# The first feed-forward layer of a two-block model as seven quarter products per weight panel

## What is computed

```python
x = x + jnp.concatenate([mix, mem_out], axis=-1) @ w_out[layer]
u = rms_norm(x, norm_ffn_g[layer]) @ w_ff1[layer]          # 1024 -> 4096
x = x + jnp.square(jax.nn.relu(u)) @ w_ff2[layer]          # 4096 -> 1024
```

## Time and profile before

| what | value |
|---|---|
| median of three runs | 1949.53 us |
| lowest and highest run | 1947.63 and 1950.62 us |
| span of the profiled execution | 1949.5 us |
| PE busy | 1872.8 us (96%) |
| DVE busy | 923.3 us (47%) |
| ACT busy | 741.2 us (38%) |
| POOL busy | 235.6 us (12%) |
| first product of the feed-forward layer | 457.4 us |
| last product of the feed-forward layer | 817.9 us |

### The profile page before, as it was taken

One profiled execution on the slowest core, in us unless ns is written; L12 is line 12 of the kernel. 1 busy time (PEld: TensorE's weight loads), 2 busy tenths in 40 slices (PEclk: granted clock), 3 DMA queues, 4 the chain that ended last, 5 costly groups with the idle time before them and its releaser, 6 DMA issues. The chain is left out here.

```text
span 1949.5 us, 32648 instructions
## 1 busy us (share of the span) xinstructions
PE 1872.8 (96%) x13677; PEld 1529.4 (78%) x13677; DVE 923.3 (47%) x1380; ACT 741.2 (38%) x1208; POOL 235.6 (12%) x295
## 2 busy tenths in 40 slices
PE   7999989889999999999999899999999999999998
PEld 6777877757888888778866688888888888888888
DVE  4446766555433444466368564343322763433223
ACT  6633444343321232245358453322222552222222
POOL 4012656410000000000124100000130000000000
PEclk9999999999999999999989999999999999999999
DMA  5222000012322322362100213223233113232222
GB/s 183 87 80 72 4 3 3 12 44 89 106 87 90 105 87 87 99 125 87 44 1 2 66 66 108 87 91 104 75 112 95 52 63 102 87 107 77 87 92 71
DMA packets 152069, 147.97 MB, mean 76 GB/s; under 512 B 13533, under 2 KB 149883, under 8 KB 151931
## 3 DMA queue, kind: packets, MB, share of 16 engines
q1 hardware_dynamic: 151804, 145.91, 23.8%
q10 hardware_dynamic: 126, 0.04, 0.0%
HBM read 143.84 MB, written 2.10 MB: 75 GB/s over the span
## 5 line engine op out<-in xcount | busy, mean ns | idle before, releaser
L243 DVE TENSOR_TENSOR weight_low<-weight_ring,weight_high 128x2048 fp32r<-128x2048 f32 (+2 forms) x141 | 301.1, 2135 | 482.6 <-ACT weight_high L234 482.5
L234 ACT CAST weight_high<-weight_ring 128x2048 fp32r<-128x2048 f32 (+2 forms) x141 | 249.9, 1773 | 320.6 <-PE psum L263 320.0
L261 PE MATMUL psum<-tail_operand_high,weight_high 128*128 128x512 f32 (+1 forms) x768 | 292.9, 381 | 8.6 <-DVE tail_operand_low L2815 7.9
L263 PE MATMUL psum<-tail_operand_high,weight_low 128*128 128x512 f32 (+1 forms) x768 | 290.7, 378 | 0.0
L262 PE MATMUL psum<-tail_operand_low,weight_high 128*128 128x512 f32 (+1 forms) x768 | 290.7, 378 | 0.0
L261 PE MATMUL psum<-tail_hidden_high,weight_high 128*128 128x512 f32 (+1 forms) x520 | 183.2, 352 | 2.5 <-DVE tail_hidden_low L3290 2.5
L263 PE MATMUL psum<-tail_hidden_high,weight_low 128*128 128x512 f32 (+1 forms) x520 | 182.7, 351 | 0.0
L262 PE MATMUL psum<-tail_hidden_low,weight_high 128*128 128x512 f32 (+1 forms) x520 | 182.6, 351 | 0.0
L261 PEld LDWEIGHTS psum<-tail_operand_high,weight_high 128*128 128x128 f32 x768 | 145.7, 190 | 39.9 <-issue 5.9
L262 PEld LDWEIGHTS psum<-tail_operand_low,weight_high 128*128 128x128 f32 x768 | 145.8, 190 | 29.8 <-issue 0.5
L263 PEld LDWEIGHTS psum<-tail_operand_high,weight_low 128*128 128x128 f32 x768 | 145.8, 190 | 29.4
(11 more groups left out here) (441 smaller groups left out, 3140.0 us busy)
## 6 DMA issues: line engine op xcount, KB each, us to landing
weight_ring<-in_w_ff SPq DMA_DIRECT2D x32, 1024.0 KB, 5.2
weight_ring<-in_ffn_w_gate SPq DMA_DIRECT2D x22, 1024.0 KB, 5.1
weight_ring<-in_ffn_w_up SPq DMA_DIRECT2D x22, 1024.0 KB, 5.1
weight_ring<-in_ffn_w_down SPq DMA_DIRECT2D x16, 768.0 KB, 4.4
weight_ring<-in_rw_in SPq DMA_DIRECT2D x11, 1024.0 KB, 5.1
weight_ring<-in_ffn_w_down SPq DMA_DIRECT2D x16, 640.0 KB, 3.9
weight_ring<-in_attn_w_in SPq DMA_DIRECT2D x9, 1024.0 KB, 5.4
weight_ring<-in_w_out SPq DMA_DIRECT2D x4, 1024.0 KB, 5.0
```

The source lines that it names most:

```text
L234: act.copy(self.w_hi[:, slot, 0:n], self.ring[:, slot, 0:n]).then_inc(self.panel_high, 1)
L243: dve.tensor_tensor(self.w_lo[:, slot, 0:n], self.ring[:, slot, 0:n], self.w_hi[:, slot, 0:n], ALU.subtract).then_inc(self.panel_low, 1)
L261: pe.matmul(out, w_hi, x_hi, start=start, stop=False)
L263: return pe.matmul(out, w_lo, x_hi, start=False, stop=stop)
```

## The change

The two multiplications of the feed-forward layer are done by a scheme of Strassen's kind (the form with seven products and fifteen sums). A panel of weights is seen as a 2x2 matrix of quarters (two blocks of input channels by two blocks of 128 output columns), the operand likewise (two blocks of channels by two halves of 256 tokens). Seven products of quarters take the place of eight.

- `Sevens` handles one panel. POOL forms four sums of quarters of the raw weights, each 128x512 (`sum_first`, `sum_second`). ACT and DVE split seven quarters and sums instead of four quarters, in four groups: 512, 1024, 1024 and 1024 columns. PE makes 7 x 4 x 3 = 84 matrix multiplications of 256 columns, in the order c = 0 to 6. ACT copies three partial results out of PSUM (`keep_first`, `keep_second`, `keep_third`), DVE adds the rest to them (`add_12`, `add_22`, `add_11`, `finish_21`). Products 2, 3 and 4 wait for the copies (`kept`), product 6 for `add_22` (`read`).
- `Turner` does the same for an operand: POOL forms four sums of quarters (128x256 each) in `turn`, ACT and DVE split seven quarters in groups of 3 and 4.
- `FirstOutput` takes the place of `project_add` for `w_out`, and makes the operand of the layer in turned form.
- `FeedForward` runs 32 panels in the order of `ffn_order`: four chunks, each of four input panels (each makes 256 hidden channels) and four output panels. For an output panel DVE scales the result (`finish_21`, `finish_22`, `finish_first`) and POOL adds it to the residual (`add_out`, two instructions of 128x512).
- The panels of `w_ff2` are now 8 blocks of rows by 256 columns per chunk. The number of weight bytes is the same.

The core of the diff (constructors, memory placement, the removed bodies of `project_add` and `squared_relu_in` and the unchanged `NormOperand` left out):

```diff
+PRODUCT_SLOT = (0, 2, 3, 5, 4, 6, 7)
+PRODUCT_GROUP = (0, 1, 1, 2, 2, 3, 3)
+PRODUCT_OPERAND = (0, 3, 4, 2, 5, 1, 6)
+PRODUCT_BANK = (0, 2, 0, 2, 0, 1, 0)
...
+    def sum_first(self, pool, pos):
...
+        self.landed(pool, pos)
+        if pos:
+            pool.wait_ge(self.low, 3 * (pos - 1) + 2)
+        pool.tensor_tensor(s1, raw[:, 0, 1], raw[:, 1, 1], ALU.add).then_inc(self.summed, 1)
+        pool.wait_ge(self.summed, 4 * pos + 1)
+        pool.tensor_tensor(s2, s1, raw[:, 0, 0], ALU.subtract).then_inc(self.summed, 1)
+
+    def sum_second(self, pool, pos):
...
+            pool.wait_ge(self.low, 3 * (pos - 1) + 3)
+        pool.tensor_tensor(s3, raw[:, 0, 0], raw[:, 0, 1], ALU.subtract).then_inc(self.summed, 1)
+        pool.wait_ge(self.summed, 4 * pos + 2)
+        pool.tensor_tensor(s4, raw[:, 1, 0], s2, ALU.subtract).then_inc(self.summed, 1)
...
+    def products(self, pe, pos, operand, claim):
...
+        for c in range(7):
+            claim(pe, c)
+            if c in (0, 1, 3):
+                pe.wait_ge(self.low, 3 * pos + PRODUCT_GROUP[c] + 1)
+            if c == 5:
+                pe.wait_ge(self.k.panel_low, self.g0 + pos + 1)
+            if c in (2, 3, 4):
+                pe.wait_ge(self.kept, 3 * pos + c - 1)
+            if c == 6:
+                pe.wait_ge(self.read, 4 * pos + 2)
+            slot = (self.base + PRODUCT_SLOT[c]) % 8
+            for kk in range(kp):
...
+                pe.matmul(out, w, x_hi, start=kk == 0 and not opened, stop=False, skip_group_check=opened)
+                pe.matmul(out, w, x_lo, start=False, stop=False, skip_group_check=opened)
+                last = pe.matmul(out, self.w_lo[:, slot, kk, :], x_hi, start=False, stop=kk == kp - 1, skip_group_check=opened)
+            last.then_inc(self.k.panel_used if c == 6 else self.done, 1)
...
+    def turn(self, pool, q, first_ready, b22_ready, b21_ready):
...
+        pool.tensor_tensor(r[:, 4], r[:, 0], r[:, 1], ALU.subtract).then_inc(self.turned, 1)
+        pool.wait_ge(*b22_ready)
+        pool.wait_ge(self.turned, 4 * q + 1)
+        pool.tensor_tensor(r[:, 5], r[:, 3], r[:, 4], ALU.subtract).then_inc(self.turned, 1)
+        pool.tensor_tensor(r[:, 6], r[:, 3], r[:, 0], ALU.subtract).then_inc(self.turned, 1)
+        pool.wait_ge(*b21_ready)
+        pool.wait_ge(self.turned, 4 * q + 2)
+        pool.tensor_tensor(r[:, 7], r[:, 2], r[:, 5], ALU.subtract).then_inc(self.turned, 1)
...
+CHUNK = 4
+CHUNKS = 4
+
+
+def ffn_order():
...
+    for c in range(CHUNKS):
+        order += [("in", p) for p in range(CHUNK * c, CHUNK * (c + 1))]
+        order += [("out", c, o) for o in range(KT // 2)]
...
+class FeedForward:
...
+    def act(self, act):
...
+            if before[0] == "in":
+                self.bend_first(act, pos - 1)
...
+            if urgent:
+                self.high(act, pair, 0)
+            if pos <= self.last:
+                c11, c12, c21, c22 = self.quarters(pos)
+                self.wait_room(act, pos)
+                sevens.keep_first(act, pos, c11)
+            if urgent:
+                self.high(act, pair, 1)
+            elif pair is not None:
+                self.high(act, pair, 0)
+            if pos <= self.last:
+                sevens.keep_second(act, pos, c22)
+                sevens.split_high(act, pos, 3)
+                sevens.keep_third(act, pos, c12)
+            if pos < self.last:
+                sevens.split_high(act, pos + 1, 0)
+                sevens.split_high(act, pos + 1, 1)
...
+            if pair is not None and not urgent:
+                self.high(act, pair, 1)
...
+            if pos < self.last:
+                sevens.split_high(act, pos + 1, 2)
...
+    def dve(self, dve):
...
+            if pos:
+                self.finish_21(dve, pos - 1)
+            if pair is not None:
+                self.low(dve, pair, 0)
+                if urgent:
+                    self.low(dve, pair, 1)
+            if pos <= self.last:
+                c11, c12, c21, c22 = self.quarters(pos)
+                sevens.split_low(dve, pos, 3)
+            if pos < self.last:
+                sevens.split_low(dve, pos + 1, 0)
+            if pos <= self.last:
+                sevens.add_12(dve, pos, c12)
+                sevens.add_22(dve, pos, c22)
+                self.finish_22(dve, pos)
+            if pos < self.last:
+                sevens.split_low(dve, pos + 1, 1)
...
+            if pos <= self.last:
+                sevens.add_11(dve, pos, c11)
+                self.finish_first(dve, pos)
+            if pair is not None and not urgent:
+                self.low(dve, pair, 1)
...
+            if pos < self.last:
+                sevens.split_low(dve, pos + 1, 2)
...
+    def pool(self, pool):
...
+            if urgent:
+                self.turn(pool, pos - 1)
+            if before[0] == "out":
+                self.add_out(pool, pos - 1)
+            if pos < self.last:
+                sevens.sum_first(pool, pos + 1)
+            if before[0] == "in" and not urgent:
+                self.turn(pool, pos - 1)
+            if pos < self.last:
+                sevens.sum_second(pool, pos + 1)
```

More of the change, by code:

```diff
@@ L1634, in __init__ @@
         if at > k.nc.sbuf_usable_end:
[L1635 to L1639, removed]
+            raise ValueError(f"the middle's operand ends at {at}")
 class MixOperand:
@@ L1651, in _ @@
             for b in range(KT):
[L1652 removed]
+                act.copy(t.mix_hi[:, b, :], t.mix[:, b, :]).then_inc(self.high, 1)
         @block.vector
@@ L1688, in halves, with __init__ @@
+class NormOperand(NormSums):
+    def __init__(self, t, name, gain, squares):
+        super().__init__(t, name, squares)
+        self.gain = gain
+        self.high, self.low = t.sems(f"{name}_operand", "high", "low")
     def halves(self, b, at=slice(None)):
@@ L1795, in squared_relu_in, with __init__, pe @@
-def squared_relu_in(k, t, block, half, x):
-    ps, name, blocks = k.ps, f"ff1{half}", 16
-    g0 = k.first_panel[name]
-    made, bent, squared, high = t.sems(name, "made", "bent", "squared", "high")
-    low, base = t.hidden_low, blocks * half
-    pair = t.take_pairs(blocks // 2)
-    @block.tensor
-    def _(pe):
-        for i in range(blocks // 2):
-            t.claim(pe, pair(i), (bent, 2 * i + 2))
-            w_hi, w_lo = k.panel(pe, g0, i // 4, i % 4, KT, PW)
+class FirstOutput:
+    def __init__(self, k, t, mix, sums, gain, sevens, turner):
+        self.k, self.t, self.mix, self.sums, self.gain, self.sevens, self.turner = k, t, mix, sums, gain, sevens, turner
+        self.g0 = k.first_panel["w_out"]
+        self.made, self.taken, self.gained = t.sems("w_out", "made", "taken", "gained")
+        self.pair = t.take_pairs(KT // 2)
+    def pe(self, pe):
+        k, t = self.k, self.t
+        for i in range(KT // 2):
+            t.claim(pe, self.pair(i), (self.taken, 2 * i + 2))
+            w_hi, w_lo = k.panel(pe, self.g0, 0, i, KT, PW)
@@ new lines, in pool, with emit, _ @@
+    def pool(self, pool):
+        for i in range(KT // 2):
+            self.turner.turn(pool, i, (self.gained, 2 * i + 1), (self.gained, 2 * i + 2), (self.gained, 2 * i + 2))
+            if i == 1:
+                self.sevens.sum_first(pool, 0)
+                self.sevens.sum_second(pool, 0)
+    def emit(self, block):
+        @block.tensor
+        def _(pe):
+            self.pe(pe)
+        @block.scalar
+        def _(act):
+            self.act(act)
+        @block.vector
+        def _(dve):
+            self.dve(dve)
+        @block.gpsimd
+        def _(pool):
+            self.pool(pool)
```

578 lines of the change are left out of this document (414 added, 164 removed).

## The result

The changed kernel takes 2034.25 us (median of four runs, 2031.73 to 2040.89) against 1948.58 us for the kernel before in the same session (1947.40 to 1950.62). The ratio is 1.0439, 95% interval 1.0419 to 1.0459. So it is slower, as forecast, by 85.7 us in place of 52.8. The profiled execution spans 2034.4 us, and what follows is read from it.

A forecast was written before the change was run, and what follows sets the result against it. The port shared by DVE and POOL was taken to bound the changed layer: 412.8 - 12 + 4 + 6.7 + 3 = 414.5 us against 361.7, so 1949.5 + 52.8 = 2002 us. The range was 1970 to 2050 us.

The forecast's parts named there:

- PE's part: Feed-forward layer: 84 multiplications per panel take 9.98 us in place of 11.25, 40.6 us gained if other engines are in time.
- DVE and POOL exclude each other: Shared SBUF port: their holdings add to floors of 13.07 us behind an input panel, 11.45 behind an output panel.
- the walk: Step by step timing of one panel: 13.3 us behind input panels, 12.0 behind output panels, 15.3 at turns; chance 0.62.
- The turns: First output panel of each chunk: product 1 waits for the turned hidden operand and ends at 6.6 us; 15.3 us each.
- My third rival: PE's clock falls to 1.2 GHz in the layer: a panel 17.9 us, the kernel about 2165 us; chance 0.05.
- The start: From w_out's last product to panel 0's T = 0: 4 us, in place of panel 0's iteration of 12.
- 16 us, hidden there: POOL's work for the turned operand and first panel's sums, 16 us, is hidden beside the w_out panels' 45 us.
- The last chunk: Its output iterations were taken at 12.0 us like the others; next operand steps counted only behind the last panel.
- The transfer: Weight transfer behind an input panel doesn't matter: slot free at 5.5, landed 5.2 us later, wanted at 11.1.
- PE stays the bound: Rival: DVE and POOL interlock less, a panel is 9.98 us, each turn adds 4 us, kernel 1930 us; chance 0.12.
- Nothing overlaps: Rival: no DVE work overlaps POOL's holdings, layer 478 us, kernel 2066 us, anything from 2035 up; chance 0.17.
- About no change: Rival: POOL holdings a quarter shorter bring the floor to 11.3 us per iteration, 1953 to 1982 us or nothing; chance 0.04.

The follow-up runs named there:

- tiny_pool: Changed kernel with POOL's weight sums and hidden operand subtractions done on one column, order and waits kept, output wrong: 1951.16 us (one run).
- held_tiny: Changed kernel with each following chunk's first input panel run before the output panels, and POOL's weight sums and hidden subtractions on one column: 1932.36 us, ratio 0.9905.
- memset_pool: Changed kernel with POOL's weight sums and hidden subtractions replaced by writes of constants that keep POOL as busy, output wrong: 1965.51 us (one run).
- extra_sum: Changed kernel with the first weight sum on POOL made twice per panel, 31 times in all: 2066.57 us, ratio 1.0598.
- filler: Changed kernel with spare 256 column multiplications into an unused bank where PE waits in each turn: 2029.19 us, ratio 1.0415.

## Why the prediction was right in its sign and low in its size

**PE's part: right.** 84 multiplications at 0.1188 us give 9.98 us, and tiny_pool and held_tiny run at 9.96 to 10.1 us per panel. The 36 loads of stationary blocks more per panel and the semaphores cost nothing beside that.

**DVE and POOL exclude each other: right, and shown.** Taking POOL's reads away gives 83 us back (tiny_pool), keeping POOL busy with writes in their place loses only 14 of them (memset_pool), and one more sum costs its holding (extra_sum). The ordinary iterations came out at 13.5, 13.5 and 12.5 us behind input panels, where the walk had 13.3, and at 12.3, 13.0, 12.2 and 11.5 behind output panels, where it had 12.0. The port rule that the prediction cited (the Trainium skill, SBUF — State Buffer, § SBUF: two separate sides) holds in these runs as well. It also says that DVE's instructions with two SBUF inputs meet the lock only against a GpSimd instruction that reads SBUF. memset_pool agrees: the 38 low parts beside writes alone take 1.22 us, the 13 beside an addition 1.67.

**The turns: mis-sized, 15.3 us predicted, 18.3 measured on average, +11.9.** This is the step "product 1 waits for four subtractions and both casts, product 1 ends at 6.6". The mechanism was right and the size off by two terms. The chain ran until 8.7 us into the turn: ACT's second cast stands behind the copy of product 0, which itself waits for the first low part, and DVE's low parts in the turn take 1.35 and 1.75 us behind POOL's subtractions and sums. tiny_pool has the same wait ending at 6.8 us, so 1.2 us of it are the port. And I had the five products behind it at full clock. PE waited 3.49 and 1.33 us within the turn and ran at 1.2 GHz from 526 to 535; filler gives 4.9 us back for the four turns. My third rival had the clock falling for the whole layer, which it did not (0.92); that it falls in stretches was in no case of mine.

The turns are not the only such stretches. The clock is 0.63 from 463.5 to 477 us, in the first iteration, and 0.50 to 0.57 for 3.4 to 6.8 us each from 496.8, 510.5, 804.6, 879.7 and 892.8. In an ordinary iteration that need not cost anything. The iteration of the third panel of the first chunk, with such a stretch, is as long as that of the third panel of the second chunk at full clock, since PE has idle time to give:

```profile
496.45:509.95 13.50, 11.73 (x84) 11.26 (x84) 12.47 (x13) 8.27 (x14) 12.64 (x9) 0.87 0.24 79
604.06:617.55 13.49, 10.58 (x86) 10.01 (x85) 12.45 (x12) 7.32 (x11) 12.69 (x9) 1.00 0.23 78
```

In a turn it does cost: the first two have their second wait end at 7.98 and 7.99 us, with clocks of 0.73 and 0.80, and last 19.0 and 17.1. The stretch from 804.6 lies in an iteration of 13.97 us in place of 13.5. What the low clock costs there, in the first iteration and in the last chunk, no run separates.

**The start: wrong, 4 us predicted, 9.8 measured.** The term that was too small is "With what stands queued for the port I take 4 us", and the step that failed is the one before it, by which the four turned groups and the first panel's sums are "16 us, hidden there". POOL had the time, but DVE is not free there. The first fence is DVE from 440 us, the second POOL:

```profile
440.66 3.25 DVE L240 TENSOR_TENSOR weight_low<-weight_ring,weight_high 128x2048 fp32r<-128x2048 f32 x1 [0.76 <-ACT weight_high L231]
443.83 2.31 DVE L1800 TENSOR_TENSOR middle_x<-middle_pairs,middle_x 128x1024 fp32r<-128x1024 f32 x1
446.06 3.48 DVE L1894 TENSOR_TENSOR middle_square_total<-middle_square_total,middle_x_squares 128x512 f32<-128x512 f32 x2
...
460.54 0.68 DVE L1992 TENSOR_TENSOR residual_T<-psum,residual_T 128x512 f32<-128x512 f32 x1
```

```profile
447.25 1.74 POOL L1659 TENSOR_TENSOR middle_sums<-weight_ring,middle_sums 128x512 f32<-128x512 f32 x1
...
462.24 0.73 POOL L1778 TENSOR_TENSOR middle_pairs<-middle_pairs 128x256 f32<-128x256 f32 x1 [7.09 <-ACT middle_pairs L1952]
```

The low part of 2048 columns takes 3.25 us in place of 2.30, the next two steps 2.31 and 3.48 where 1.22 and 1.37 (two of 0.68) would do: 4.2 us late on DVE by 449.5. The addition of an output block of `w_out` at 460.54 then stands behind low parts and a sum of squares that are not wanted as soon, and POOL waits 7.09 us for what follows from it. Both parts can be told from the runs. Without the reads of the weight sums (tiny_pool, memset_pool, held_tiny) the stretch is 6.5 us, so 3.4 of the 5.8 are the weight sums on the port. The order on DVE is the same in those three; that it makes the other 2.5 is read from the timeline, and no run changed it.

**The last chunk: left out, +5.9.** In its output iterations the next operand is made (L1920, and the sums of squares, L1894), and these have two SBUF inputs as well. I had put them on the path only behind the last panel. DVE, then PE, at the end of the first of the two iterations:

```profile
873.89 2.45 DVE L1920 SCALAR_TENSOR_TENSOR middle_operand_low<-residual_T,columns_b,middle_operand_high 128x512 fp32r<-128x512 f32 x2
876.26 0.68 DVE L1894 TENSOR_TENSOR middle_square_total<-middle_square_total,mixer_mixed 128x512 f32<-128x512 f32 x1
876.87 1.21 DVE L1692 TENSOR_TENSOR weight_low<-middle_sums,weight_high 128x1024 fp32r<-128x1024 f32 x1
```

```profile
878.13 0.39 PE L1716 MATMUL psum<-middle_hidden_high,weight_high 128*128 128x256 f32 x1 [2.08 <-DVE weight_low L1692]
```

The low part that PE waits for stands behind them. tiny_pool shows the same shape with less to collide with (12.8 and 11.6 in place of 10.0), held_tiny too (12.9 and 11.6).

**The transfer: "doesn't matter" was almost right.** POOL's first sum waits 14.5 us for it in total, 6.46 us of that in the second iteration, at 481.86. That iteration overran by 2.0 us, and no other carries a loss that I can put down to a transfer.

**What would show it.** Right: PE at 82% in the layer (75 to 80% predicted), POOL near 80% (78), POOL's sums at 1.3 to 2.4 us, the low parts over 1.22, products 2 and 3 waiting for ACT's copies, the longest waits in the turns (5.7 us and three of 3.5, though one of 4.2 stands in the first iteration), starts 0.119 us apart wherever the clock is full. Wrong: DVE "near 100%". It is at 77% over the layer and 92% in input iterations, because it waits for ACT's high parts (37.3 us for one group alone), which in part wait for POOL's sums. The port is the bound, and it can be taken while each of its users shows idle time.

**The rivals.** "PE stays the bound" needed a mean iteration under 11.2 us; it is (892.65 - 468.26) / 31 = 13.7. Its price for a turn, 4 us over a panel, was too low as well: without the sums it is 6 to 8.6. "Nothing overlaps" had 15.8 and 14.05 us per iteration; the ordinary ones lie 0.1 and 0.8 us over the floors of 13.07 and 11.45 on average (13.17 and 12.26 in the second chunk). A single iteration can lie under its floor, as those of 12.5 do; the eight of a chunk have a floor of 98.1 us and took 105.6 to 108.3. "About no change" had a slip: 11.3 us is the floor with cheaper holdings behind input panels alone, 13.07 less a quarter of 6.92. Behind output panels the same gives 9.7, less than PE's 9.98, so its 1953 us was too high. Nothing measured here rests on it.

## What to carry to other kernels

- Before moving elementwise work to POOL, add up per iteration the time in which DVE's instructions with two SBUF inputs and POOL's reading ones hold the port. That sum is a floor like an engine's busy time, and neither engine's own share shows it.
- A scheme that saves multiplications and adds dependent steps must be priced at its turns, start and end on their own: here 23 ordinary iterations together came out within 3 us of the walk, and the rest of the 32 us lay in four turns, the start and the last chunk.
- Where PE waits in a turn, count the products behind it at the lower clock, and look at what is queued ahead of the wanted cast on ACT.

## What the runs showed of the hardware beyond that

- POOL writing constants (955 ns for 128x1024) doesn't hinder DVE's low parts, which have two SBUF inputs: 1.22 us for 1024 columns beside writes alone, as beside a POOL that does almost nothing.
- PE's granted clock fell behind two waits, 1.83 and 3.49 us, that end at 521.37 and 526.17, behind two iterations in which PE was busy 84% of the time, part of it already at a lower clock (0.87 over both). The starts stood 0.21 to 0.22 us apart from 526 to 535 us, across another wait of 1.33. From 541 to 579, with 3.3 us idle in all in 37.5, the clock stayed at 1.00. It stayed there from 604 to 629 too, with PE busy 17.9 of 25 us and waits of 2.15 and 2.10 us, where the same panels of the first chunk, behind a wait of 2.21, had the stretch at 0.57.
